# First expert started from the token blocks in SBUF, its weights loaded ahead of the routing, slot lists from two one-hot tables

## Chip, cores, metric

The kernel runs on one core of a Trainium2 chip. The metric is the device time of one execution in microseconds (us), the median of several runs.

## What is computed

Two transformer blocks on 512 tokens of width 1024, in float32. The part that the change touches is the mixture of experts of the first block: a router picks a group of four experts and two experts in it, and each token's result is the gated sum of the two.

```python
def hier_moe(h, w_rg, b_rg, w_re, b_re, w_gate, w_up, w_down):
    t = h.reshape(B * S, D)
    g_logits = (t @ w_rg) + b_rg
    g_idx = jnp.argmax(g_logits, axis=-1)
    e_sel = jnp.take_along_axis(e_logits, g_idx[:, None, None], axis=1)[:, 0]
    top_v, top_i = lax.top_k(e_sel, EXPERT_TOP_K)
    ...
    hid = jax.nn.silu(jnp.einsum('td,edf->tef', t, w_gate)) * jnp.einsum('td,edf->tef', t, w_up)
    hid = hid * gates.astype(hid.dtype)[:, :, None]
    y = jnp.einsum('tef,efd->td', hid, w_down)
```

There are 16 experts, each with 1024 x 512 gate and up weights and 512 x 1024 down weights.

## The kernel before

Products of weights are made from two parts of each operand, a rounded one (`hi`) and the rest (`lo`), in three matmuls of type float32r. ScalarE makes the `hi` part of a weight chunk (L160), VectorE the `lo` part (L164); plain float32 products and transposes occur in the routing. T = 512 tokens are NT = 4 blocks of P = 128; D = 1024 is KC = 8 chunks. Order is set by each engine's own instruction list and by semaphores that count.

**Routing.** When x is complete (L1885), TensorE turns the four token blocks to rows with products against the gain diagonals (`turn_scaled`, L1149), adds the shift (`add_shift`, L1234), and ScalarE evicts each block to `h_tok` (L710). SP stores each block to `h_dram` (L474). Meanwhile VectorE works out the two choices of each token in a chain of small linked steps (L1906 to L1941), TensorE counts for each expert how many tokens stand before a token (L1241, L1243), and VectorE makes from that `pos1`, the gates, and `tok_table` (six fields for each block and expert: token number, destination row, two gate parts and ones).

**Slots.** An expert takes up to 128 tokens in a round; the number of rounds is computed (`rounds`), and every engine reads it before its loop over rounds (`value_load`). This input needs one round. In it VectorE makes for each of the 16 experts a one-hot of positions (L2009), and TensorE multiplies it with the table (L1316, L1323) to get the list of tokens. `slot_numbers` (L2015 to L2025) turns the lists of experts 0 and 1, and later those of the rest, into row numbers. GpSimd gathers the rows of an expert from `h_dram` by an indirect DMA (L2406).

**Experts.** `turn_tokens` (L1257) transposes the gathered rows, ScalarE and VectorE split them into `e_hi` (L724) and `e_lo` (L1966). `expert_in` (L1267 to L1269) multiplies four weight chunks for the gate and four for the up half, `turn_hidden` (L1276) and `expert_down` (L1287 to L1289) follow one expert later. Results are evicted (L739) and scattered to `y_dram` by GpSimd (L2414). A ring of 12 buffers holds the weight chunks of 512 KB; SP loads them (L153) once a buffer's previous chunk is split, all inside its loop over rounds, behind the token stores. The ring lies over `h_hi`, `h_lo` and `raw`, which are free once x is complete. After the experts SP loads the rows of `y_dram`, VectorE adds the two choices (L2057) and TensorE turns them back (L1356).

## Time and profile before

| | us |
|---|---|
| median of 3 runs | 1859.93 |
| lowest and highest | 1853.70, 1861.27 |
| the profiled execution | 1857.48 |
| its span | 1855.7 |
| TensorE busy in the span | 1790.5 (96%) |
| VectorE, ScalarE, GpSimd busy | 1216.3, 913.3, 184.6 |

The profile is one execution. A window row gives each engine's busy time in a stretch, TensorE's granted clock as a share of full speed (1.00 is 2.4 GHz, 0.50 is 1.2 GHz) and what the DMA engines moved. PE is TensorE, DVE VectorE, ACT ScalarE, POOL GpSimd, SP SyncE. A matmul in float32 shows as two instructions.

### The profile page before, as it was taken

The numbers are of one execution on the slowest core, as the hardware profiler recorded it, in microseconds if no ns is written. First come the engines' busy times: TensorE is split into PE (matmuls) and PEld (weight loads), VectorE is DVE, ScalarE is ACT, GpSimd is POOL, SyncE is SP. The second block draws the span as 40 slices with busy tenths as digits, with TensorE's granted clock in tenths as the row PEclk, the third lists the DMA queues.
The fourth block names the chain that finished last, engine by engine and source line by source line (L and its number), as shares of the span: only waits on it lengthen the run. The fifth ranks groups of instructions, "written<-read, shape, count | busy, mean of one in ns | idle before, by whom it ended". The sixth has DMA issues, their size and how long they took to land.

```text
span 1855.7 us, 26079 instructions
## 1 busy us (share of the span) xinstructions
PE 1790.5 (96%) x8478; PEld 1393.8 (75%) x8478; DVE 1216.3 (66%) x1892; ACT 913.3 (49%) x1395; POOL 184.6 (10%) x219
## 2 busy tenths in 40 slices
PE   7999989899999879999999999999998999999999
PEld 5777667788888657776788888887774788888887
DVE  6777784798898672554577777224998567777422
ACT  3566752578788534564444444115665543444310
POOL 0000000222322100001000000000764000000000
PEclk9999999799999989999999999999999999999999
DMA  9533132999999452111233233331221223232321
GB/s 400 184 97 103 57 126 80 345 363 376 378 375 372 156 200 74 57 57 32 83 102 100 92 100 108 97 101 46 69 68 30 73 81 100 94 98 92 123 90 57
DMA packets 74099, 261.60 MB, mean 141 GB/s; under 512 B 10536, under 2 KB 10664, under 8 KB 72752
## 3 DMA queue, kind: packets, MB, share of 16 engines
q1 hardware_dynamic: 69424, 252.33, 38.8%
q0 software_dynamic: 4608, 8.40, 1.2%
q8 instruction: 40, 0.66, 0.1%
q14 instruction: 27, 0.22, 0.0%
HBM read 256.47 MB, written 12.60 MB: 145 GB/s over the span
## 4 chain that ended last, share of the span: by engine, by line
PE 86%; DVE 5%; DMA 3%; ACT 3%; issue 2%; SPq 0%; POOL 0%; DVEq 0%; POOLq 0%; ACTq 0%
PE ps L1027 19%; PE ps L1029 19%; PE ps L1028 19%; PE ps L1267 3%; PE ps L1269 3%; PE ps L1268 3%; PE ps L1660 2%; PE ps L1089 2%; PE ps L1287 2%; PE ps L1289 2%; PE ps L1288 2%; PE ps L1110 1%; DMA raw<-in_w_a 1%; PE ps L991 1%; PE ps L1480 1%
## 5 line engine op out<-in xcount | busy, mean ns | idle before, releaser
L1027 PE MATMUL ps<-h_hi,w_hi 128*128 128x512 f32 x1120 | 447.7, 400 | 1.3 <-DVEq L2273 1.3
L1029 PE MATMUL ps<-h_hi,w_lo 128*128 128x512 f32 x1120 | 436.8, 390 | 0.0
L1028 PE MATMUL ps<-h_lo,w_hi 128*128 128x512 f32 x1120 | 436.3, 390 | 0.0
L125 DVE TENSOR_TENSOR w_lo<-raw,w_hi 128x1024 fp32r<-128x1024 f32 x212 | 265.9, 1258 | 186.0 <-ACT w_hi L120 185.7
L120 ACT ACTIVATE w_hi<-raw 128x1024 fp32r<-128x1024 f32 x212 | 221.4, 1049 | 201.8 <-PE ps L1029 164.0
L1027 PEld LDWEIGHTS ps<-h_hi,w_hi 128*128 128x128 f32 x1120 | 210.4, 188 | 66.9 <-issue 24.3
L1029 PEld LDWEIGHTS ps<-h_hi,w_lo 128*128 128x128 f32 x1120 | 210.2, 188 | 44.5
L1028 PEld LDWEIGHTS ps<-h_lo,w_hi 128*128 128x128 f32 x1120 | 210.5, 188 | 43.7 <-issue 2.4
L164 DVE TENSOR_TENSOR w_lo<-ring,w_hi 128x1024 fp32r<-128x1024 f32 x128 | 149.5, 1218 | 28.0 <-ACT w_hi L160 28.0
L911 ACT ACTIVATE tmp<-ps,param 128x512 f32<-128x512 f32 x88 | 68.6, 780 | 185.6 <-DVE ps L2239 185.6
L2247 DVE SCALAR_TENSOR_TENSOR tmp<-ps,param,tmp 128x511 f32<-128x511 f32 (+1 forms) x176 | 131.8, 749 | 18.9 <-DVE tmp L2247 3.0
L1027 PE MATMUL ps<-gv_hi,w_hi 128*128 (+1 forms) x352 | 139.1, 395 | 0.0
L1029 PE MATMUL ps<-gv_hi,w_lo 128*128 (+1 forms) x352 | 139.0, 395 | 0.0
L1028 PE MATMUL ps<-gv_lo,w_hi 128*128 (+1 forms) x352 | 139.0, 395 | 0.0
L160 ACT ACTIVATE w_hi<-ring 128x1024 fp32r<-128x1024 f32 x128 | 128.6, 1055 | 11.8 <-PE ps L1269 11.8
L2383 POOL TENSOR_TENSOR pool_carrier<-const 128x1 f32<-128x1 f32 x74 | 35.3, 477 | 701.7 <-DVE x L2271 427.0
L2239 DVE TENSOR_TENSOR ps<-ps,const 128x512 f32<-128x512 f32 x88 | 61.2, 696 | 63.5 <-PE ps L1029 63.4
L2474 POOL TENSOR_TENSOR part<-prod,part 128x512 f32<-128x512 f32 x64 | 84.9, 1327 | 55.4 <-ACT prod L959 51.0
L1267 PE MATMUL ps<-w_hi,e_hi 128*128 128x512 f32 x192 | 78.4, 409 | 2.7 <-DVE e_lo L1966 2.7
L1029 PEld LDWEIGHTS ps<-gv_hi,w_lo 128*128 128x128 f32 x352 | 66.0, 187 | 16.2
L1027 PEld LDWEIGHTS ps<-gv_hi,w_hi 128*128 128x128 f32 x352 | 66.0, 187 | 16.1
L1028 PEld LDWEIGHTS ps<-gv_lo,w_hi 128*128 128x128 f32 x352 | 66.0, 187 | 16.1
(345 smaller groups left out, 2916.8 us busy)
## 6 DMA issues: line engine op xcount, KB each, us to landing
ring<-in_w_m SPq DMA_DIRECT2D x192, 512.0 KB, 5.6
raw<-in_w_b SPq DMA_DIRECT2D x180, 512.0 KB, 3.5
raw<-in_w_a SPq DMA_DIRECT2D x32, 512.0 KB, 3.8
ada_late<-in_ada_b SPq DMA_DIRECT2D x32, 512.0 KB, 4.6
ada<-in_ada_a SPq DMA_DIRECT2D x8, 1024.0 KB, 17.1
y_tok<-y_dram SPq DMA_DIRECT2D x8, 512.0 KB, 8.0
x<-in_x SPq DMA_DIRECT2D x2, 1024.0 KB
h_dram<-h_tok SPq DMA_DIRECT2D x4, 512.0 KB, 2.6
```

What stands on the lines that cost most here:

```text
L120: act.activation(self.hi[:, s, :], self.raw[:, s, :], ACT.Copy).then_inc(self.hi_done, 1)
L125: dve.tensor_tensor(self.lo[:, s, :], self.raw[:, s, :], self.hi[:, s, :].bitcast(F32), ALU.subtract).then_inc(self.lo_done, 1)
L160: act.activation(self.hi[c % PARTS_M], self.ring[:, c % RING], ACT.Copy).then_inc(self.hi_done, 1)
L164: dve.tensor_tensor(self.lo[c % PARTS_M], self.ring[:, c % RING], self.hi[c % PARTS_M].bitcast(F32), ALU.subtract).then_inc(self.lo_done, 1)
L911: act.activation(tmp[:, c], ps[:, c], ACT.Identity, scale=PR_at("ffn_w", it, 6, 3 * p + (f * 2 + val) * 3 * FC + 2), bias=PR_at("ffn_b", i ...
L1027: pe.matmul(dst, hi, a_hi, start=first, stop=False, skip_group_check=True)
L1028: pe.matmul(dst, hi, a_lo, start=False, stop=False, skip_group_check=True)
L1029: return pe.matmul(dst, lo, a_hi, start=False, stop=last, skip_group_check=True)
L1267: pe.matmul(ps[:, bank], e_hi[:, k], hi, start=(k == 0), stop=False, skip_group_check=True)
L2239: dve.tensor_tensor(ps[:, c], ps[:, c], r_kept, ALU.mult).then_inc(z_done, 1)
L2247: dve.scalar_tensor_tensor(out=tmp[:, c, back:], in0=ps[:, c, 0:T - back], scalar=PR_at("ffn_w", it, 6, 3 * p + (f * 2 + val) * 3 * FC + tap),
L2474: pool.tensor_tensor(part[:, p], prod[:, n % 4], part[:, p], ALU.add).then_inc(part_step, 1)
```

## The change

The table gets five fields for each of the two choices, block and expert: the token number, the destination row, a one, and two gate parts, each times the choice's expert one-hot. One one-hot for each choice (position of a token in its expert, whichever that is) times this table gives the lists of all 16 experts in 8 products with 80 columns. The first expert's tokens aren't gathered by a DMA: a third one-hot, `first_of`, is multiplied with `h_tok`, which gives them already turned, in two halves that are split one by one. SP issues the first expert's 12 weight loads ahead of the round count, with the four token stores among them, and waits for one more list at the end; GpSimd gathers from expert 1 on. Part of the last token block's products and ScalarE's exponentials stand earlier. The lists and one-hots of a next round are made at the end of the loop. `first_turned`, `first_hi` and `first_lo` are existing semaphores under new names; in SBUF the table and one-hots take room of `h_tok_at`, which lay unused. Cut to what the prediction speaks of:

```diff
--- before.py
+++ after.py
@@ -150,7 +151,8 @@
     def load(self, sp, base, i, c):
 
         sp.wait_ge(self.lo_done, base + (c + 1))
-        sp.dma_start(self.ring[:, c], self.src[bass.ds(i, 1), c]).then_inc(self.loaded[c][0], 16)
+        src = self.src[i:i + 1, c] if isinstance(i, int) else self.src[bass.ds(i, 1), c]
+        sp.dma_start(self.ring[:, c], src).then_inc(self.loaded[c][0], 16)
 
     def split_hi(self, act, base, lap, c):
 
...
@@ -469,18 +478,33 @@
             sp.dma_start(s_dram.rearrange("o (p k) -> p (o k)", k=KC), mod[:, 3 * KC:4 * KC]).then_inc(shift_in, 16)
             sp.wait_ge(shift_in, 16)
             sp.dma_start(shift_read[:], s_dram.broadcast_to([P, D])).then_inc(shift_in, 16)
-            for t in range(NT):
+
+            def store_tokens(t):
                 sp.wait_ge(h_tok_done, t + 1)
                 sp.dma_start(h_dram[t * P:(t + 1) * P], h_tok[:, t]).then_inc(h_stored, 16)
 
+            for c in range(8):
+                sm.load(sp, 0, 0, c)
+            store_tokens(0)
+            store_tokens(1)
+            for c in (8, 9):
+                sm.load(sp, 0, 0, c)
+            store_tokens(2)
+            store_tokens(3)
+            for c in (10, 11):
+                sm.load(sp, 0, 0, c)
             sp.wait_ge(rounds_done, 1)
             n_rounds = sp.value_load(rounds[0:1, 0:1], min_val=1, max_val=NT)
-            with sp.Fori(0, n_rounds) as r:
-                with sp.Fori(0, NE) as i:
-                    for c in range(RING):
-                        sm.load(sp, r * (12 * NE) + i * 12, i, c)
-
+            with sp.Fori(1, n_rounds * NE) as n:
+                e = n & (NE - 1)
+                sp.lower_val(e)
+                for c in range(RING):
+                    sm.load(sp, n * 12, e, c)
+
+            slots_end = n_rounds + 1
+            sp.lower_val(slots_end)
             sp.wait_ge(y_free, n_rounds * NE + 2)
+            sp.wait_ge(slots_done, slots_end)
             for t in range(NT):
                 for choice in range(2):
                     row = choice * T + t * P
@@ -709,9 +733,9 @@
                 act.wait_ge(h_turned, t + 1)
                 act.activation(h_tok[:, t].rearrange("p (b c) -> p b c", b=2), ps[:, turned_at(t):turned_at(t) + 2], ACT.Copy,
                                scale=r_tok[:, t:t + 1]).then_inc(h_tok_done, 1)
-                if t in (1, 2):
-                    act.wait_ge(route_sel, t)
-                    act.activation((r44[:, 1], r4[:, 9])[t - 1], (r44[:, 0], r4[:, 8])[t - 1], ACT.Exp).then_inc(route_exp, 1)
+                if t < 2:
+                    act.wait_ge(route_sel, t + 1)
+                    act.activation((r44[:, 1], r4[:, 9])[t], (r44[:, 0], r4[:, 8])[t], ACT.Exp).then_inc(route_exp, 1)
...
@@ -758,7 +782,11 @@
                 base, lap = r * (12 * NE), r * NE
                 for c in range(AHEAD_M):
                     sm.split_hi(act, base, lap, c)
-                expert_tokens_hi(r * NE)
+                    if c == 1:
+                        act.wait_ge(first_turned, r + 2)
+                        act.activation(e_hi[:, 0:KC // 2].rearrange("p k c -> p (k c)"), ps[:, 0], ACT.Copy).then_inc(first_hi, 1)
+                act.wait_ge(e_turned, r * NE + 3)
+                act.activation(e_hi[:, KC // 2:].rearrange("p k c -> p (k c)"), ps[:, 1], ACT.Copy).then_inc(e_hi_done, 1)
                 for c in range(8):
                     sm.split_hi(act, base, lap, c + AHEAD_M)
...
@@ -1237,6 +1265,9 @@
 
             add_shift(0)
             add_shift(1)
+            pe.wait_ge(h_tok_done, 1)
+            for k in range(KC // 2):
+                turn_scaled(k, 3)
             pe.wait_ge(route_sel, 3)
             pe.matmul(ps[:, RB, 0:NT * NE], C("before"), r16[:, 0], start=True, stop=False, skip_group_check=True)
             for d in range(1, NT + 1):
@@ -1244,10 +1275,19 @@
                                  stop=(d == NT), skip_group_check=True)
             last.then_inc(router_mm, 1)
             add_shift(2)
-            pe.wait_ge(h_tok_done, 1)
-            for k in range(KC):
+            for k in range(KC // 2, KC):
                 turn_scaled(k, 3)
             add_shift(3)
+
+            def slots_of(made):
+                pe.wait_ge(onehot_done, made)
+                for b in range(2 * NT):
+                    last = pe.matmul(ps[:, SSQ, 0:NE * FIELDS], onehot[:, b // NT, b % NT],
+                                     tok_table[:, b].rearrange("p e f -> p (e f)"), start=(b == 0), stop=(b == 2 * NT - 1),
+                                     skip_group_check=True)
+                last.then_inc(slots_done, 1)
+
+            slots_of(2)
 
             def turn_tokens(pair, n, s):
 
@@ -1257,9 +1297,25 @@
                     last = pe.transpose(ps[:, k // 4, k % 4 * P:(k % 4 + 1) * P], e_x[s][:, k * P:(k + 1) * P], C("ident"))
                 last.then_inc(e_turned, 1)
 
-            def expert_in(base, c0, bank):
+            def gather_first(r):
+
+                n = r * NE
+                pe.wait_ge(h_tok_done, NT)
+                pe.wait_ge(onehot_done, r * 3 + 3)
+                pe.wait_ge(e_lo_done, n + 1)
+                for b in range(2):
+                    for t in range(NT):
+                        for j in range(KC // 2):
+                            k = b * (KC // 2) + j
+                            last = pe.matmul(ps[:, b, j * P:(j + 1) * P], h_tok[:, t, k * P:(k + 1) * P], first_of[:, t].bitcast(F32),
+                                             start=(t == 0 and j == 0), stop=(t == NT - 1), skip_group_check=True)
+                    last.then_inc(e_turned if b else first_turned, 1)
+
+            def expert_in(base, c0, bank, second_half=None):
 
                 for b in range(4):
+                    if b == 2 and second_half is not None:
+                        pe.wait_ge(e_lo_done, second_half)
                     sm.ready(pe, base, c0 + b)
                     for j in range(2):
                         hi, lo = sm.parts(c0 + b, j, FE)
...
 
-                pe.wait_ge(y_evicted, r * NE + 1)
...
                 n = r * NE
-                turn_tokens(r * (NE // 2), n, 0)
-                with pe.Fori(6, NE // 2) as m:
-                    slots_of(m)
-                pe.wait_ge(e_lo_done, n + 2)
+                gather_first(r)
+                pe.wait_ge(first_lo, r + 5)
                 pe.wait_ge(silu_done, n + 1)
-                expert_in(r * (12 * NE), 0, 2)
+                expert_in(r * (12 * NE), 0, 2, n + 2)
                 pe.wait_ge(hid_done, n + 1)
                 expert_in(r * (12 * NE), 4, 3)
                 turn_tokens(r * (NE // 2), n + 1, 1)
                 with pe.Fori(0, NE // 2 - 1) as m:
                     pe.wait_ge(e_lo_done, r * NE + m * 2 + 3)
-                    expert_pe(r, m * 2 + 1, r * (NE // 2) + m + 1, 1)
+                    expert_pe(r, m * 2 + 1, r * (NE // 2 - 1) + m, 1)
                     pe.wait_ge(e_lo_done, r * NE + m * 2 + 4)
                     expert_pe(r, m * 2 + 2, r * (NE // 2) + m + 1, 0)
                 pe.wait_ge(e_lo_done, r * NE + (NE + 1))
                 expert_pe(r, NE - 1, 0, 1)
                 turn_hidden(r * NE + (NE - 1))
                 expert_down(r * (12 * NE), 12 * NE - 4, r * NE + (NE - 1))
+                slots_of(r * 3 + 6)
 
             pe.wait_ge(sm.used, n_rounds * (12 * NE) + PARTS_M)
...
@@ -1910,9 +1946,20 @@
                 link(dve.tensor_tensor(onehot_out, key, over(key_max, 2, T4), ALU.is_equal))
 
             TN, TE = [P, NT, NG + NE], [P, NT, NE]
-            tok = over(C("tok"), 2, TE)
-            link(dve.tensor_copy(tok_table[:].rearrange("p t e f -> p (t e f)"), ones[:, 0:1].broadcast_to([P, NT * NE * 6])))
...
 
-            link(dve.scalar_tensor_tensor(out=tok_table[:, :, :, 1], in0=r16[:, 2], scalar=float(T), in1=tok, op0=ALU.mult,
-                                          op1=ALU.add))
+            link(dve.tensor_tensor(fields(0), chosen_twice, for_both(numbers[:].rearrange("p f n t -> p f (n t)")), ALU.mult))
+            link(dve.tensor_copy(tok_table[:, :, :, 2], chosen))
+            dve.wait_ge(route_exp, 2)
+            link(dve.tensor_reduce(out=r4[:, 2], in_=r44[:, 1], axis=AX.X, op=ALU.add))
+            link(dve.scalar_tensor_tensor(out=r4[:, 10], in0=r4[:, 9], scalar=1.0, in1=r4[:, 2], op0=ALU.add, op1=ALU.mult))
+            link(dve.reciprocal(gates[:, 0], r4[:, 10]))
+            link(dve.tensor_tensor(gates[:, 1], gates[:, 0], r4[:, 9], ALU.mult))
+            gate = gates[:].rearrange("p n t -> p (n t)")
+            link(dve.tensor_copy(gate_parts[:, 0], gate))
+            link(dve.tensor_tensor(gate_parts[:, 1], gate, gate_parts[:, 0].bitcast(F32), ALU.subtract))
+            link(dve.tensor_tensor(fields(3), chosen_twice, for_both(gate_parts[:].bitcast(F32)), ALU.mult))
 
             dve.wait_ge(router_mm, 2)
+            link(dve.scalar_tensor_tensor(out=pos_of[:].rearrange("p n t e -> p n (t e)"),
+                                          in0=ps[:, RB, 0:NT * NE].unsqueeze(1).broadcast_to([P, 2, NT * NE]), scalar=1.0,
+                                          in1=r16[:, 1:3].rearrange("p n t e -> p n (t e)"), op0=ALU.add, op1=ALU.mult))
+            link(dve.tensor_reduce(out=pos[:].rearrange("p n t -> p (n t)"), in_=pos_of[:].rearrange("p n t e -> p (n t) e"),
+                                   axis=AX.X, op=ALU.add))
+
+            link(dve.tensor_tensor(pos_first, pos_of[:, 0, :, 0], pos_of[:, 1, :, 0], ALU.add))
+
+            def slots_wanted():
+                for n in range(2):
+                    dve.tensor_tensor(onehot[:, n], over(pos[:, n], 2, [P, NT, P]), over(iota_r[:], 1, [P, NT, P]),
+                                      ALU.is_equal).then_inc(onehot_done, 1)
+
+            def first_wanted():
+                dve.tensor_tensor(first_of[:], over(pos_first, 2, [P, NT, P]), over(iota_r[:], 1, [P, NT, P]),
+                                  ALU.is_equal).then_inc(onehot_done, 1)
+
+            dve.wait_ge(iota_done, 1)
+            slots_wanted()
             link(dve.tensor_reduce(out=rounds_f[:, 0:1], in_=ps[:, RB, NT * NE:(NT + 1) * NE], axis=AX.X, op=ALU.max))
             link(dve.tensor_scalar(rounds_f[:, 1:2], rounds_f[:, 0:1], float(P), 1.0, ALU.is_gt, ALU.add))
             for n in (2, 3):
                 link(dve.scalar_tensor_tensor(out=rounds_f[:, n:n + 1], in0=rounds_f[:, 0:1], scalar=float(n * P),
                                               in1=rounds_f[:, n - 1:n], op0=ALU.is_gt, op1=ALU.add))
             dve.tensor_copy(rounds[:], rounds_f[:, 3:4]).then_inc(rounds_done, 1)
-            dve.wait_ge(route_exp, 2)
-            link(dve.tensor_reduce(out=r4[:, 2], in_=r44[:, 1], axis=AX.X, op=ALU.add))
-            link(dve.scalar_tensor_tensor(out=r4[:, 10], in0=r4[:, 9], scalar=1.0, in1=r4[:, 2], op0=ALU.add, op1=ALU.mult))
-            link(dve.reciprocal(r4[:, 11], r4[:, 10]))
-            link(dve.tensor_tensor(r4[:, 3], r4[:, 11], r4[:, 9], ALU.mult))
-            link(dve.tensor_tensor(pos1[:], r16[:, 1], over(r4[:, 11], 2, TE), ALU.mult))
-            link(dve.tensor_tensor(r16[:, 1], r16[:, 2], over(r4[:, 3], 2, TE), ALU.mult))
-            link(dve.tensor_tensor(r16[:, 2], pos1[:], r16[:, 1], ALU.add))
-            link(dve.tensor_copy(tok_table[:, :, :, 2], r16[:, 2]))
-            link(dve.tensor_tensor(tok_table[:, :, :, 4], r16[:, 2], tok_table[:, :, :, 2].bitcast(F32), ALU.subtract))
-            link(dve.scalar_tensor_tensor(out=pos1[:], in0=ps[:, RB, 0:NT * NE].rearrange("p (t e) -> p t e", t=NT),
-                                          scalar=1.0, in1=r16[:, 0], op0=ALU.add, op1=ALU.mult))
+            first_wanted()
 
             def expert_tokens_lo(n):
...
                 base = r * (12 * NE)
-                with dve.Fori(2, 6) as m:
-                    slots_of(m)
-                slots_of(6)
+                dve.wait_ge(slots_done, r + 1)
+                dve.wait_ge(idx_ready, r * (2 * NE - 1) + 1)
+                dve.tensor_copy(slot_table[:].rearrange("p e f -> p (e f)"), ps[:, SSQ, 0:NE * FIELDS]).then_inc(slot_idx, 1)
+                dve.wait_ge(slot_idx, r * 3 + 1)
+                dve.scalar_tensor_tensor(out=slot_rows_f[:], in0=over(slot_table[:, :, 2], 1, [P, 2, NE]), scalar=-4096.0,
+                                         in1=slot_table[:, :, 0:2].rearrange("p e f -> p f e"), op0=ALU.mult, op1=ALU.add)\
+                   .then_inc(slot_idx, 1)
+                dve.wait_ge(slot_idx, r * 3 + 2)
+                dve.tensor_scalar(slot_rows[:], slot_rows_f[:], 4096.0, None, ALU.add).then_inc(slot_idx, 1)
+                dve.tensor_tensor(slot_gate[:], slot_table[:, :, 3], slot_table[:, :, 4], ALU.add)
                 sm.split_lo(dve, base, 0)
-                slots_of(7)
-                expert_tokens_lo(r * NE)
-                for c in range(1, 4):
-                    sm.split_lo(dve, base, c)
-                dve.wait_ge(slots_done, r * NE + (NE + 2))
-                slot_numbers(SSQ, 2, NE, 3)
-                dve.tensor_scalar(iota_r[:], iota_r[:], float(P), None, ALU.add).then_inc(iota_done, 1)
-                dve.wait_ge(iota_done, r + 2)
+                sm.split_lo(dve, base, 1)
+                dve.wait_ge(first_hi, r + 2)
+                dve.tensor_tensor(e_lo[:, 0:KC // 2].rearrange("p k c -> p (k c)"), ps[:, 0],
+                                  e_hi[:, 0:KC // 2].bitcast(F32).rearrange("p k c -> p (k c)"), ALU.subtract).then_inc(first_lo, 1)
+                sm.split_lo(dve, base, 2)
+                dve.wait_ge(e_hi_done, r * NE + 1)
+                dve.tensor_tensor(e_lo[:, KC // 2:].rearrange("p k c -> p (k c)"), ps[:, 1],
+                                  e_hi[:, KC // 2:].bitcast(F32).rearrange("p k c -> p (k c)"), ALU.subtract).then_inc(e_lo_done, 1)
+                sm.split_lo(dve, base, 3)
                 for c in range(4, 8 + AHEAD_M):
                     sm.split_lo(dve, base, c)
                 hidden(base, 7, r * NE, 0)
@@ -2049,6 +2094,10 @@
                     expert_dve(r, e)
                 expert_dve(r, NE - 1)
                 hidden_lo(r * NE + (NE - 1))
+                dve.tensor_scalar(iota_r[:], iota_r[:], float(P), None, ALU.add).then_inc(iota_done, 1)
+                dve.wait_ge(iota_done, r + 2)
+                first_wanted()
+                slots_wanted()
 
...
@@ -2392,7 +2441,6 @@
             pool.wait_ge(rounds_done, 1)
             n_rounds = pool.value_load(rounds[0:1, 0:1], min_val=1, max_val=NT)
             pool.wait_ge(zeroed, 2)
-            pool.wait_ge(h_stored, 16 * NT)
 
             def column(ap, e):
...
@@ -2403,6 +2451,8 @@
                 pool.tensor_copy(src_e[:, s:s + 1], column(slot_src, e)).then_inc(idx_ready, 1)
                 pool.wait_ge(idx_ready, copied)
                 settle(1)
+                if isinstance(e, int) and e == 1:
+                    pool.wait_ge(h_stored, 16 * NT)
                 pool.indirect_dma_start(e_x[s][:], None, h_dram, bass.IndirectOffsetOnAxis(ap=src_e[:, s:s + 1], axis=0),
                                         bounds_check=T - 1, oob_is_err=False).then_inc(fetched[s], 16)
```

## Rows read from the trace of the kernel before

**Rows 1.** Stage windows: from:to, length, each engine's busy us (instructions), granted clock, DMA share, GB/s.
```profile
324.00:326.50 2.50, 0.07 (x1) 0.00 (x0) 0.93 (x3) 1.11 (x1) 0.00 (x0) 1.00 0.19 77
326.50:350.50 24.00, 21.60 (x84) 20.07 (x85) 18.28 (x30) 9.16 (x9) 5.87 (x11) 0.50 0.91 355
...
360.00:362.60 2.60, 0.00 (x0) 0.00 (x0) 2.06 (x3) 2.60 (x3) 1.54 (x4) 1.00 1.03 411
400.00:600.00 200.00, 200.00 (x930) 162.94 (x929) 178.01 (x165) 161.69 (x178) 53.54 (x85) 1.00 0.99 376
...
637.50:640.50 3.00, 3.00 (x8) 2.32 (x8) 0.00 (x0) 0.00 (x0) 0.31 (x2) 0.50 0.14 56
```

**Rows 2.** Chain of waits, two experts: start, us, what.
```profile
603.74 0.44 PE ps L1276 x4
...
621.84 0.44 PE ps L1276 x4
```

**Rows 3.** Chain of waits, from the routing's end to the first expert matmul.
```profile
324.00 0.23 DVE pos L1961
...
325.80 0.70 DVE onehot L2009
...
331.68 8.09 DMA e_x<-h_dram,src_e
...
339.81 1.97 PE ps L1257 x8
...
345.28 0.79 PE ps L1267
```

**Rows 4.** Timeline of TensorE, experts 0 and 1: start, us, instruction [idle before, releaser].
```profile
350.55 0.39 PE L1267 MATMUL ps<-w_hi,e_hi 128*128 128x512 f32 x1
...
358.92 1.04 PE L1257 MATMUL ps<-const,e_x 128*128 128x128 f32 x8
362.62 0.50 PE L1267 MATMUL ps<-w_hi,e_hi 128*128 128x512 f32 x1 [2.66 <-DVE e_lo L1966]
```

**Rows 5.** Timeline of the token blocks on TensorE and ScalarE.
```profile
315.66 0.59 PE L1234 MATMUL ps<-e_y,tmp 128*128 128x512 f32 x1
...
317.46 0.43 PE L1241 MATMUL ps<-r,const 128*128 128x64 f32 x2 [1.21 <-DVE r L1939]
...
320.40 1.05 PE L1149 MATMUL ps<-e_silu,x 128*128 128x128 f32 x8
...
321.29 1.06 PE L1149 MATMUL ps<-e_hid,x 128*128 128x128 f32 x8
...
324.10 1.11 ACT L710 ACTIVATE h_tok<-ps,e_y 128x1024 f32<-128x1024 f32 x1 [2.30 <-PE ps L1234]
```

**Rows 6.** Timeline of VectorE: a step of 64 and one of 512 elements.
```profile
317.18 0.23 DVE L1939 TENSOR_TENSOR r<-r 128x64 f32<-128x64 f32 x1
...
327.66 0.69 DVE L2009 TENSOR_TENSOR onehot<-pos,iota_r 128x512 fp32r<-128x512 f32 x1 [0.57 <-PE ps L1316]
```

**Rows 7.** Instructions on the ring (ns min/median/max, first and last start), and ScalarE's table load.
```profile
L160 ACT ACTIVATE w_hi<-ring x128: 1040/1054/1064, 332.0 to 627.9; 128x1024 fp32r<-128x1024 f32 x128
L164 DVE TENSOR_TENSOR w_lo<-ring,w_hi x128: 1212/1218/1237, 339.7 to 629.8; 128x1024 fp32r<-128x1024 f32 x128
...
330.73 1.28 ACT L160 ACT_TABLE_LOAD   x1 [5.51 <-DMA ring<-in_w_m]
```

**Rows 8.** When x is ready (timeline), the weight loads' landing, and the stores' (DMA issues).
```profile
307.94 0.75 DVE L1885 SCALAR_TENSOR_TENSOR x<-ps,mod,x 128x512 f32<-128x512 f32 x1 [6.62 <-PE ps L1029]
...
DMA to landing us min/median/max: 3.7/5.6/13.6
...
h_dram<-h_tok SPq DMA_DIRECT2D x4, 512.0 KB, 2.6
```

**Rows 9.** The gathers' time to landing.
```profile
DMA to landing us min/median/max: 3.6/6.1/8.4
```

**Rows 10.** Waits between 634 and 656 us: engine, line, awaited, us, times, longest.
```profile
PE ps L1356 <- DVE y_tok L2057: 11.6, 1, 11.6
```

92 lines of the change are left out of this document (33 added, 59 removed).

## Prediction

> **What bounds the kernel now.** I read the stage windows first: they show where TensorE is full and where not. Over 400 to 600 us TensorE is busy for 200.00 of 200 us at full clock [rows 1]. The experts there repeat every 621.84 - 603.74 = 18.10 us [rows 2], which is 72 matmuls of 0.233 us plus transposes, so the expert loop is bound by TensorE. Nothing ahead of it changes its rate; what comes ahead only moves its start. The part that isn't bound by work is 324 to 362.6 us, the way into the experts. The chain of waits over it [rows 3] is a relay of small steps: the loop's entry on VectorE, a one-hot, its products, the slot numbers, GpSimd's preparations, an 8.09 us gather, the transposes, and only then the first expert matmul at 345.28. TensorE's granted clock is 0.50 (the 1.2 GHz level) for the 24 us from 326.5 to 350.5, after 2.5 us with almost no work, and comes back at 350.5, after 12 of the expert matmuls ran at it [rows 1, 3, 4]. The last wait of the stage is at 358.9 to 362.6, while the tokens of expert 1 are turned and split [rows 4]. From 362.62 on TensorE has no gap until the last expert's tail near 634. So the change is worth the distance by which that 362.62 moves, as long as no later expert meets a new wait.
>
> **The change, part by part.** I follow TensorE and take each other engine as cover.
>
> (a) The last token block. The products of tokens 384 to 511 (L1149, 8 products in 16 instructions) stand behind the counts and after the third shift; they start at 320.40 and 321.29, so 8 instructions take 0.89 us, 0.111 each [rows 5]. Half of them, 0.89 us, go ahead of the counts. TensorE is through with the second block at 315.66 + 0.59 = 316.25 and waits until 317.46 for the chosen experts, so they fit into 1.21 us and cost nothing; without that cover they would delay the counts by 0.89 us. The last block's eviction then starts at 323.2 instead of 324.10 and, with its 1.11 us, is done at 324.3.
>
> (b) VectorE's new tables. They must be done when TensorE wants them. Prices: 64 elements 0.23 us, 512 elements 0.69 us [rows 6]; by the line through them 128 take 0.30 and 256 take 0.43, and a linked step adds about 0.04. From 317.3, behind the sum of the chosen experts [rows 6]: two field products of 256 (0.47 each), a copy of 128 (0.33), four gate steps and two splits of tiny size (0.2 each, 1.2), the positions and their sum (0.33 each), the first expert's positions (0.2). That is 3.3 us, 320.7. Two one-hots of 512 (1.3) end at 322.0, the five tiny steps of the round count (0.9) at 322.9, the first expert's one-hot at 323.6. The exponentials stand one block earlier on ScalarE, the second behind the second block's eviction (316.3 + 1.11 [rows 5]) and not behind the third's, so it is there before 318 and VectorE does not wait for it. TensorE wants the first two one-hots at 323.2 and the third at 324.3 or later: 1.2 and 0.7 us of cover. If the five-word stride made the 256-element steps cost 0.69 each, 0.5 us would be gone and still nothing late.
>
> (c) Slot lists. Sixteen one-hots and 64 products, in the old loop until 345.28, become 8 products with 80 columns. No row shows 80 columns in this type. L1149's instructions have 128 columns and are nearest: 8 x 0.111 = 0.9 us; as pairs they would be 1.8. I take 1.0 (bounds 0.9 and 1.8): 324.2.
>
> (d) Loop entry. VectorE needs 1.57 us from the end of its last operation (324.23) to the first of the loop (325.80), most of it loading the round count [rows 3]. ScalarE and TensorE do the same. For TensorE the trace doesn't show it alone: bounds are 0 (its sequencer does it while the queued products run) and 1.5 us. Rounds are known at 322.9, before its queue is empty, so I take the middle, 0.7 us behind 324.3: the gather starts at 325.0.
>
> (e) Gather by products. 2 banks x 4 token blocks x 4 chunks = 32 float32 products. Each such product is two instructions in the trace (the 8 of L1149 are 16), so 64, with L1149's shape: 64 x 0.111 = 7.1 us and 0.2 for the first one's way in, 7.3, ending at 332.3 [rows 5]. It replaces the DMA gather (8.09) and the transposes (1.97 at half clock) [rows 3]. Bounds: 7.1, and 8.4 if each takes the 0.131 that the busy 1.05 us of 8 give; at half clock, 14.6.
>
> (f) First expert's input products. ScalarE enters at 324.3 + 1.5, table load 1.28, then splits of 1.05 and subtractions of 1.22 on VectorE [rows 7]. By that order the first token half is split at about 331.4, behind two weight chunks and ahead of 332.3, and the second at about 333.7, when TensorE wants it at 335.1; the later chunks are ready 1.6 us or more before their use. So 48 matmuls (8 chunks x 6) run without a gap: 48 x 0.233 = 11.2 us, to 343.5. Before they took 358.92 - 345.28 = 13.6: the first 12 took 350.55 - 345.28 = 5.3, 0.44 each, the other 36 took 8.4, 0.233 each [rows 3, 4].
>
> (g) Expert 1. Turn, ScalarE's copy, VectorE's subtraction: the same 362.62 - 358.92 = 3.7 us as before [rows 4], to 347.2. VectorE's other splits up to chunk 11 end at about 344.3 and its hidden product at 345.0, before that subtraction wants to start at 345.5; 0.5 us to spare.
>
> Sum: 362.62 - 347.2 = 15.4 us earlier, carried through the expert loop to the end.
>
> (h) SP. It now issues 12 loads of 512 KB once x is ready, at 307.94 + 0.75 = 308.7, and not behind the round count [rows 8]; the four token stores stand among them, with 8 loads ahead of the first. Before, a store landed in 2.6 us [rows 8]. 14 transfers of 0.524 MB up to the last store at 355 GB/s (326.5 to 350.5 us, loaded [rows 1]) are 1.48 us each: 20.7 us, plus the 2.6 of a store, 332.0. GpSimd holds only the gather of expert 1 for it; issue 0.6 later, landing 8.4 at most [rows 9]: 341.0, wanted at 343.5. Cover is 2.5 us. Chunks 0 to 9 land before ScalarE wants them; expert 1's loads are issued from 329 on, one as each chunk is split, 12 ahead of use as before. The Trainium skill, "DMA: Bandwidth & Descriptors", section on queues, rings and completion order, says that each DMA engine takes one ring's descriptors in ring order. By that rule the stores can't pass the weights, and this would give the late gather among the rivals; the rows of before hold no store behind loads that could confirm it.
>
> (i) Loop end. Three one-hots (2.0 us) on VectorE behind the last hidden split and 8 products behind TensorE's last expert matmul. TensorE has no work for 11.6 us there, since it waits for VectorE's sum of the loaded rows [rows 10]; SP's added wait is met within 1 us of the last expert matmul, before the last result is even scattered. Cost nothing; without that cover, 3 us.
>
> Total: 1857.48 - 15.4 = 1842.1. That profiled execution lies 2.4 us below the median of the three runs, inside their 1853.7 to 1861.3.
>
> **Rivals.**
> 1. The clock falls. For: 2.5 us without work preceded the fall at 326.5, and a short gap near 634 preceded the 3 us at 0.50 from 637.5 [rows 1]. Against: in the new order TensorE is without work for at most about 1.5 us there, and the 2.6 us at 360 were followed by no fall. If it falls ahead of the gather and comes back after 12 of the 48 matmuls, as before: +7.3 and 12 x 0.2 = +2.4, 1851.8.
> 2. Slower than before: the same fall, but the clock stays down for 24 us as it did at 326.5. Then the gather takes +7.3 and the 48 matmuls run at 0.44 (+9.9), 17.2 in all, expert 1 starts at 364.4 and the time is 1859.3. It is slower than before once more than 15.4 us are lost, that is when at least 40 of the 48 matmuls run at half clock.
> 3. The gather of expert 1 comes late. With a landing of 13.6 us, the longest of the weights [rows 8], it is there at 346.2: +2.7, 1844.8.
> 4. The change hides what is hidden anyway: if ScalarE's entry or VectorE's tables end last, TensorE stalls ahead of the products. Entries a further 2 us late would give 1844.
> 5. The gap of 2 us at 634 falls on another moment of the clock: the 3 us at half clock there cost 1.6. 8 matmuls at 0.44 and not 0.233. It may be spared (1840.5), or the 2.6 us gap ahead of expert 1 may bring a fall (+2.4, 1844.5).
>
> **How the numbers follow.** Forecast, with the small variants 4 and 5 around it: 0.80. Rival 1: 0.08. Rival 2: 0.03. Rival 3: 0.09. Low end: TensorE's entry free (0.7), the end gap spared (1.6), and 3.8 for the scatter of runs (the lowest lies 3.8 below the profiled one): 1836. High end: entry of 1.5 (+0.8), products at 0.131 (+1.1), rival 3 or a fall ahead of expert 1 (+2.5), slower slot lists (+0.8), the highest run's 3.8 above: 1851.1; rounded up into rival 1, 1852. A measurement here tells 0.5%, 9.3 us, from no change. Faster by over 0.5%: the forecast and rival 3 but for what the scatter takes, 0.83. Within: rivals 1 and 2 and that scatter, 0.14. Slower: 0.03, a form of rival 2 that costs 24 us, for which no row speaks.
>
> **What would show it.** Right: in the profile after, the 64 gather instructions start at 324.2 to 325.7 and take 7 to 8.4 us; the first expert matmul is at about 332.3; granted clock 1.00 from 312 to 350; weight loads begin at about 309; expert 1's first matmul is at about 347.2; the period of an expert stays 18.1. Wrong: a granted clock of 0.50 between 325 and 345; TensorE waiting on the expert 1 gather or on a weight chunk; an onehot wait ahead of 324; any gap in 350 to 600; a longer distance from the last expert matmul to the first transposes of the sum.

## The result, and the profile of the changed kernel

| | before | changed | predicted |
|---|---|---|---|
| median, us | 1859.78 | 1839.14 | 1842.1 |
| lowest to highest | 1853.7 to 1861.3 | 1838.6 to 1841.4 | 1836 to 1852 |
| ratio to before | 1 | 0.9901 (0.9882 to 0.9919) | 0.992 |
| profiled execution | 1857.48 | 1838.63 | |
| its span | 1855.7 | 1836.8 | |

The medians differ by 20.6 us and the profiled executions by 18.9, where the sum gave 15.4. The forecast's time, 1842.1, counts from the profiled execution of before, which lies 2.3 us below before's median here; so the measured time is 3.0 us below the forecast, while the gain of the medians is 5.2 us above it. The table follows both profiles along the same instructions of TensorE.

| TensorE, us | before | changed | gained so far |
|---|---|---|---|
| first router product (L1137, now L1165) | 308.74 | 308.26 | 0.5 |
| expert 1's first matmul | 362.62 | 346.75 | 15.9 |
| first matmul after the last expert's last wait | 635.95 | 620.50 | 15.5 |
| first transpose of the summed rows | 654.96 | 638.01 | 17.0 |
| first product of the next stage | 677.50 | 659.35 | 18.2 |
| end of the span | 1855.7 | 1836.8 | 18.9 |

From the router product to expert 1 it is 53.88 us before and 38.49 after, 15.39 less: the forecast's 15.4. What lies over it came elsewhere, and the rest of this section and the runs say how much of that is the change's.

The chain of waits of the changed kernel over the routing and the first expert (start, us, what):

```profile
322.72 1.12 ACT h_tok L734
323.84 0.80 issue
324.64 7.41 PE ps L1310 x64
332.05 0.24 PE ps L1323
...
343.21 0.89 PE ps L1297 x8
344.12 1.03 ACT e_hi L748
345.18 1.24 DVE e_lo L2030
...
346.75 0.71 PE ps L1323
```

The relay of [rows 3] is gone. Between the last token block and the first expert matmul stand an entry of 0.80 us and the 64 gather instructions, and from 332.05 to 343.21 the 48 matmuls follow without a gap. The stage windows, with the columns of [rows 1]:

```profile
324.00:325.50 1.50, 0.86 (x7) 0.86 (x8) 0.52 (x3) 0.75 (x1) 0.00 (x0) 1.00 1.04 426
325.50:334.00 8.50, 8.50 (x69) 8.09 (x68) 5.67 (x8) 6.94 (x9) 2.39 (x8) 1.00 1.00 391
334.00:345.00 11.00, 10.08 (x48) 8.07 (x46) 10.37 (x10) 9.14 (x10) 1.96 (x4) 1.00 0.91 323
346.80:350.40 3.60, 3.60 (x9) 2.83 (x10) 1.87 (x2) 1.00 (x2) 0.00 (x0) 0.53 1.04 380
400.00:600.00 200.00, 200.00 (x934) 163.67 (x933) 179.41 (x168) 161.78 (x178) 52.51 (x82) 1.00 0.99 376
```

Where [rows 1] had 24 us at a granted clock of 0.50, it is 1.00 from 308 to 346.8. In this profile the clock falls behind the wait ahead of expert 1 (0.53 in 346.8 to 350.4), which it did not do in before's; e5 and e10 take that up. The experts fill TensorE as before, with 934 instructions in 200 us where there were 930.

Timeline of VectorE and TensorE: a step of the new table, the one-hots, the lists:

```profile
316.83 0.62 DVE L1988 TENSOR_TENSOR tok_table<-r,numbers 128x256 fp32r<-128x256 f32 x1
...
320.52 1.29 DVE L2011 TENSOR_TENSOR onehot<-pos,iota_r 128x512 fp32r<-128x512 f32 x2
...
322.12 1.38 PE L1285 MATMUL ps<-tok_table,onehot 128*128 128x80 f32 x8
...
322.58 0.68 DVE L2015 TENSOR_TENSOR first_of<-pos_first,iota_r 128x512 fp32r<-128x512 f32 x1
```

GpSimd's timeline at the gather of expert 1, and the DMA issues between 305 and 350 us:

```profile
331.47 1.23 POOL L2456 DMA_INDIRECT e_x<-h_dram,src_e  x1 [5.00 <-DMA h_dram<-h_tok]
```

```profile
ring<-in_w_m SPq DMA_DIRECT2D x26, 512.0 KB, 7.1
h_dram<-h_tok SPq DMA_DIRECT2D x4, 512.0 KB, 7.0
```

GpSimd waits 5.00 us for the last token store. A store takes 7.0 us among the weight loads, where it took 2.6 before [rows 8]; the gather of expert 1 is nevertheless issued at 331.47, 11.7 us ahead of the transposes that read it, and the gathers of this stretch land in 7.3.

### The profile page after: what moved, and what is told of

Same layout as the page of the kernel before. It is cut to its first block, busy times and chain, and to the rows that moved or that the text cites. A ratio compares the mean times of both kernels' runs of the same rounds, so it can differ in the third digit from the quotient of the medians.

```text
span 1836.8 us, 25944 instructions
## 1 busy us (share of the span) xinstructions
PE 1779.8 (97%) x8486; PEld 1385.9 (75%) x8486; DVE 1209.8 (66%) x1882; ACT 913.2 (50%) x1396; POOL 183.0 (10%) x215
## 4 chain that ended last, share of the span: by engine, by line
PE 85%; DVE 6%; issue 4%; ACT 3%; DMA 2%; DVEq 0%; SPq 0%; POOL 0%; POOLq 0%; ACTq 0%
PE ps L1055 19%; PE ps L1057 18%; PE ps L1056 18%; PE ps L1323 3%; PE ps L1324 3%; PE ps L1325 3%; PE ps L1117 2%; PE ps L1345 2%; PE ps L1343 2%; PE ps L1344 2%; PE ps L1696 1%; PE ps L1138 1%; DMA raw<-in_w_a 1%; PE ps L1019 1%; DVE w_lo L126 1%
## 5 line engine op out<-in xcount | busy, mean ns | idle before, releaser
L2296 DVE SCALAR_TENSOR_TENSOR tmp<-ps,param,tmp 128x511 f32<-128x511 f32 (+1 forms) x176 | 131.8, 749 | 17.5 <-DVE tmp L2296 3.1
```

The costliest lines, as they stand in the source:

```text
L2296: dve.scalar_tensor_tensor(out=tmp[:, c, back:], in0=ps[:, c, 0:T - back], scalar=PR_at("ffn_w", it, 6, 3 * p + (f * 2 + val) * 3 * FC + tap),
```

## The experiments

Each run is read at two places: the median against before on the same chip, and the distance D from the first router product to expert 1's first matmul, which leaves out what executions scatter elsewhere. D is 53.88 us before and 38.49 in the changed kernel. "Per expert" is the distance between the hidden transposes of two experts, as in [rows 2].

| | median, us | ratio (95%) | D, us | per expert, us |
|---|---|---|---|---|
| e1 loads late | 1846.15 | 0.9941 (0.9924 to 0.9958) | 43.24 | 18.02 |
| e2 DMA gather | 1850.38 | 0.9957 (0.9940 to 0.9973) | 47.47 | 18.02 |
| e3 lists only | 1848.41 | 0.9951 (0.9934 to 0.9967) | 47.42 | 18.02 |
| e4 before, loads early | 1855.49 | 0.9988 (0.9976 to 1.0000) | 51.85 | 18.09 |
| e5 changed again | 1839.61 | 0.9907 (0.9892 to 0.9922) | 38.57 | 18.02 |
| e6 gather twice | 1847.73 | 0.9951 (0.9936 to 0.9966) | 45.75 | 18.02 |
| e7 tiles moved | 1843.06 | 0.9922 (0.9908 to 0.9935) | 38.55 | 18.10 |
| e8 clock kept | 1841.18 | 0.9915 (0.9901 to 0.9928) | 38.71 | 18.02 |
| e9 clock kept again | 1839.84 | 0.9909 (0.9895 to 0.9922) | 38.67 | 18.02 |
| e10 changed a third time | 1842.12 | 0.9916 (0.9902 to 0.9930) | 38.58 | 18.02 |

Before has 1857.81 on the chip of e1 to e4, 1857.61 on that of e5 to e8 and 1857.0 on that of e9 and e10.

The theory: the gain is the way into the experts, and its largest part is the product gather in place of the store, gather, transposes and half clock. The first rival: the fresh slot lists alone bring most of it. The second: the early loads are mere cover, or on the contrary carry a share.

### Loads back behind the round count (e1)

```diff
-            for c in range(8):
-                sm.load(sp, 0, 0, c)
-            store_tokens(0)
...
+            for t in range(NT):
+                store_tokens(t)
             sp.wait_ge(rounds_done, 1)
             n_rounds = sp.value_load(rounds[0:1, 0:1], min_val=1, max_val=NT)
+            for c in range(RING):
+                sm.load(sp, 0, 0, c)
```

> The changed kernel, but the first expert's 12 weight loads are issued behind the round count (about 324.2 us) and the four token stores ahead of them. Theory (the gain is the relay that is gone; the early loads only make room for it): weight chunk 1 then lands at about 329.5, the first token half is split at 332.3 in place of 330.1, and TensorE's first expert matmul moves from 331.8 to about 332.3; later chunks stay just ahead of TensorE. 0.5 to 1.5 us slower than the changed kernel, about 1840. Rival (the early loads carry the gain, since they start 16.7 us earlier): 10 us or more slower, 1849 or above.

Measured: D is 43.24, 4.75 us more than in the changed kernel. That is a miss. TensorE's timeline of this run, and behind it the chain of waits:

```profile
336.05 0.49 PE L1317 MATMUL ps<-w_hi,e_hi 128*128 128x512 f32 x1 [3.03 <-DVE e_lo L2076]
...
348.88 1.04 PE L1291 MATMUL ps<-const,e_x 128*128 128x128 f32 x8
```

```profile
324.26 1.12 ACT h_tok L728
...
331.20 13.28 DMA ring<-in_w_m
...
348.57 1.07 ACT m_hi L162
...
351.47 1.22 DVE e_lo L2024
...
353.03 0.49 PE ps L1317
```

The router product is at 309.79 here and at 308.26 in the changed kernel, so times are taken from it. TensorE is late by itself: the first expert matmul stands at 26.26 us and not at 23.54 (2.72 more), since the split of the first token half waits behind two weight chunks; behind that wait of 3.03 us the clock falls (0.54 in 337.5 to 341.2), and from the first matmul to the turn it is 12.83 and not 11.25 (1.58 more). From the turn to expert 1 it is 4.15 and not 3.70 (0.45 more).

The chain says what ended last. The tenth of the 12 loads, issued one behind another on SP, lands at 344.5. In the list of VectorE's work the splits of the first expert's chunks stand ahead of the subtraction `e_lo` for expert 1, so that subtraction begins 41.68 us behind the router product and not 36.92. No matmul stands on the chain from that landing to expert 1, so a TensorE in time would by this chain not have started expert 1 sooner; no run tries it. The early loads are worth 4.75 us once the gather is fast. The expectation priced the first matmul's delay at 0.5 us, and neither the fall nor the place of expert 1's subtraction behind the splits.

### First expert gathered by DMA, loads early or late (e2, e3)

```diff
-                gather_first(r)
+                pe.wait_ge(h_tok_done, NT)
+                pe.wait_ge(fetched[0], r * (NE // 2) * 16 + 16)
+                pe.wait_ge(e_lo_done, n + 1)
+                for k in range(KC):
+                    last = pe.transpose(ps[:, k // 4, k % 4 * P:(k % 4 + 1) * P], e_x[0][:, k * P:(k + 1) * P], C("ident"))
...
-                for e in range(1, 4):
+                for e in range(4):
                     gather(r, e, e % 2, done + (e + 1))
```

e3 has the edit of e1 as well, so that of the change the lists are left, with the earlier products and exponentials and the tokens' split in two halves.

> The changed kernel, but expert 0's tokens come by an indirect DMA and transposes as before; early loads and slot lists stay. Theory: the token stores stand behind eight weight loads and land at about 331.4, so the gather starts at 331.5 and lands 6 to 8 us later; the first expert matmul is at about 341.8 in place of 331.8, and the granted clock falls meanwhile (2.4 us more): 10 to 12.5 us slower than the changed kernel, 1849 to 1852. Rival (the DMA gather hides, since the slot rows are there 4 us earlier): at most 4 us slower, 1843.

> Only the slot lists of the change: two one-hots and the table over experts, with expert 0 gathered by DMA and its loads behind the round count. Theory: stores land at 326.5, gather from 326.9 with 12 loads in the queues beside it, 8 us, to 335; first expert matmul about 338.8 (before: 345.3), clock fallen as before: 6 to 7 us faster than the kernel before, about 1848 to 1851, and faster than the kernel with early loads and DMA gather, since there the stores wait. Rival (all lies in the clock or in the loads): within 2 us of the kernel before.

The chain of waits of e2, and behind it that of e3:

```profile
324.85 1.12 ACT h_tok L734
325.99 6.60 DMA h_dram<-h_tok
...
333.48 4.51 DMA e_x<-h_dram,src_e
...
340.71 0.79 PE ps L1323
341.50 0.43 PE ps L1324
```

```profile
322.55 1.12 ACT h_tok L728
323.69 2.58 DMA h_dram<-h_tok
...
327.16 8.05 DMA e_x<-h_dram,src_e
...
337.94 0.79 PE ps L1317
338.72 0.43 PE ps L1318
```

In both D is 47.4, 9.0 us more than with products and 6.4 less than before. The store and the gather take 11.1 us in one and 10.6 in the other: with early loads the last store is slow (6.60) and the gather quick (4.51), with late loads it is the other way round (2.58 and 8.05). TensorE has no work for 12.48 and 12.00 us ahead of the transposes, and behind that both run their first eleven to thirteen matmuls at 0.43 us, half clock. That D agrees within 0.05 us is partly luck: e3's first expert matmul is 0.47 us earlier, measured from the router product, and its 48 matmuls take 0.42 longer. The expectation that e3 is the faster one, since the stores don't wait, is a miss by D; its median is 2.0 us lower, within what medians of one kernel scatter. The Trainium skill, "DMA: Bandwidth & Descriptors", section on queues, rings and completion order, says that an engine works through one ring's descriptors in ring order; a last store of 6.60 us behind loads against 2.58 with none ahead fits it, though these runs don't tell that order from busy engines that are merely shared.

### The early loads added to the kernel before (e4)

```diff
+            for c in range(8):
+                sm.load(sp, 0, 0, c)
+            store_tokens(0)
...
             sp.wait_ge(rounds_done, 1)
             n_rounds = sp.value_load(rounds[0:1, 0:1], min_val=1, max_val=NT)
-            with sp.Fori(0, n_rounds) as r:
```

> The kernel before with the early loads alone (the stores among them as in the changed kernel). Theory: nothing on the relay waits for weights; the stores land about when the first gather is issued (331.7), and that gather has fewer loads beside it (6 in place of 8.1 us): 0 to 2 us faster than before, 1857 to 1859. Rival (the early loads carry the gain): 8 us or more faster, 1851 or below.

Measured: D falls by 2.03 us, the median by 2.3; the interval ends at 1.0. That is the upper edge of what was expected. The chain goes through the old relay still:

```profile
331.23 0.70 DVE onehot L2022
...
343.85 1.88 PE ps L1336 x8
...
346.49 0.43 PE ps L1281
```

The gather is no longer on it. In before TensorE made slot products while it waited and stood idle for the gather only at the very end:

```profile
339.81 1.97 PE L1257 MATMUL ps<-const,e_x 128*128 128x128 f32 x8 [0.73 <-DMA e_x<-h_dram,src_e]
```

So a gather that lands sooner (4.7 us here, 8.09 before) can give little more than 0.73 us before the products and their one-hots end last. The first expert matmul comes 1.13 us earlier, measured from the router product (35.41 against 36.54), and the 48 matmuls take 12.74 and not 13.64.

By D the change comes apart so: the lists with the earlier token block alone 6.46 us; the product gather without early loads another 4.18; the early loads then 4.75; together 15.39. Of the 6.46 some 0.9 are probably the token block, since e3's chain goes through its store and its eviction ends 15.59 us behind the router product where before had 16.48; no run separates the two, nor what the split in halves gives. In another order the parts have other prices: the early loads first 2.03, then the lists 4.38, then the product gather 8.98. So the theory's "largest part" holds for the gather only where the loads are early, and neither rival holds alone. The early loads are worth nothing with a DMA gather (e2 against e3, 0.05) and 4.75 with the product gather: the two parts need each other.

### The gather made twice (e6), the changed kernel beside it (e5)

```diff
-                for b in range(2):
+                for b, again in ((0, 0), (0, 1), (1, 0), (1, 1)):
...
-                    last.then_inc(e_turned if b else first_turned, 1)
+                    if again:
+                        last.then_inc(e_turned if b else first_turned, 1)
```

> The changed kernel itself, as the base for the three that follow. In its profile the first expert-1 matmul comes 38.5 us after the first router product behind the complete x (308.26 to 346.75 in the first profile), the last expert's wait 273.75 us later (or 272.2 if the clock doesn't fall at the start of expert 1). About 1839.

> The changed kernel with the 64 gather instructions issued twice (the second pass gives the same sums). Theory (the gather's products are on the path, ScalarE and VectorE wait for them): the first expert matmul moves by the 7.2 us that 64 instructions took, 1846. Rival (weight splits on ScalarE and VectorE set the start, the products run beside them): less than 4 us, 1843 or below.

```profile
325.39 0.88 issue
326.27 14.55 PE ps L1310 x128
```

128 instructions take 14.55 us where 64 took 7.41, 0.114 each. D grows by 7.2 us and the median by 8.1. So the products stand on the path with their whole length, and the rival of weight splits that set the start falls. A longer gather can't show how little the rest lies behind it. For that there is e1, and in the changed kernel VectorE was free only 0.51 us before it could begin the subtraction for expert 1, near the 0.5 of the prediction.

### The shorter period of an expert (e7)

The changed kernel needs 18.02 us for an expert and before 18.09, though its loop is the same. TensorE's timeline of before, then of the changed kernel, first and last of the 12 gate and up matmuls that read `m_hi` or `m_lo`:

```profile
582.70 0.39 PE L1267 MATMUL ps<-m_hi,e_hi 128*128 128x512 f32 x1
...
585.26 0.39 PE L1269 MATMUL ps<-m_lo,e_hi 128*128 128x512 f32 x1
```

```profile
585.46 0.39 PE L1323 MATMUL ps<-m_hi,e_hi 128*128 128x512 f32 x1
...
587.97 0.40 PE L1325 MATMUL ps<-m_lo,e_hi 128*128 128x512 f32 x1
```

Eleven steps take 2.56 us in one and 2.51 in the other, 0.233 and 0.228 each. The matmuls that read `w_hi` and `w_lo` take 0.233 in both. By the tiles that the change makes smaller, `m_hi` and `m_lo` lie 416 words (1664 bytes of each partition) lower. e7 puts them back with a tile that nobody reads:

```diff
+            sb("m_at", [P, 416], stack=st)
             m_hi = sb("m_hi", [P, PARTS_M - SLOTS, 1024], F32R, stack=st)
```

> The changed kernel with 416 unused words ahead of m_hi, so that m_hi and m_lo lie where they lay before the change. Theory (where these two lie sets the pitch of the matmuls that read them, 0.229 us in the changed kernel and 0.233 before): an expert takes 18.09 us and not 18.02, the stretch of the experts 273.3 us where no clock fall is in it and not 272.2; 1.1 us slower, 1840. Rival (the shorter period comes from the other order of transfers): period stays 18.02 and the time 1839.

The chain of waits of e7, then of the changed kernel, at the hidden transposes:

```profile
573.27 0.44 PE ps L1333 x4
...
591.37 0.44 PE ps L1333 x4
```

```profile
570.36 0.44 PE ps L1332 x4
...
588.37 0.44 PE ps L1332 x4
```

The period goes back to 18.10. Fifteen experts times 0.07 are 1.1 us of the gain which come from where tiles lie. The stretch from expert 1 to the last expert's wait agrees: 273.33 us before and 272.22 in e5, both without a fall of the clock; 274.64 in e7 and 273.75 in the changed kernel, both with one. The median of e7 is 3.4 us above e5's and its 1843.06 a miss against the expected 1840; the excess lies within what the changed kernel's own medians scatter (e10). The unread tile moves `e_x1` and `e_y1` too, which lie behind `m_lo`; that `m_hi` and `m_lo` matter is read from the matmuls, of which only those that read them change their step. Why the address matters isn't settled by these runs.

### The clock kept up (e8, e9) and the changed kernel a third time (e10)

The fall behind expert 1's wait is in the changed kernel's first profile and in e10, and not in e5, which is the same kernel. The windows of e5 and e10:

```profile
346.80:350.40 3.60, 3.02 (x13) 2.48 (x14) 2.72 (x4) 1.93 (x2) 0.13 (x1) 1.00 1.04 379
```

```profile
346.80:350.40 3.60, 3.04 (x7) 2.46 (x8) 2.48 (x3) 0.93 (x2) 0.11 (x1) 0.57 1.02 390
```

With the fall the stretch from expert 1 to the last expert's wait took 273.72 to 273.75 us (changed, e2, e10), without it 272.21 to 272.22 (e1, e3, e5, e6): 1.5 us. The length of the wait doesn't decide it: in e1 it is 3.12 us and no fall follows, in e5 2.67 and none, in e10 2.67 and one. e8 gives TensorE products that nobody reads in four of its waits (`unread(n)` issues n of them):

```diff
                 turn_tokens(r * (NE // 2), n + 1, 1)
+                pe.wait_ge(silu_done, n + 2)
+                unread(2)
...
                 turn_hidden(r * NE + (NE - 1))
+                unread(2)
...
             pe.wait_ge(y_evicted, n_rounds * NE + 1)
+            unread(11)
...
+                if t:
+                    for _ in range(4):
+                        pe.matmul(ps[:, 2, (NT - 1) * P:], C("ident"), const[:, 0:P], start=True, stop=True,
+                                  skip_group_check=True)
```

> The changed kernel with matmuls whose results nobody reads in the waits of TensorE: two 512-column float32 products ahead of expert 1 and two ahead of the last down products, eleven ahead of the sum's transposes and four of 128 columns between its token blocks. Theory (the half clock after these waits costs 1.5 us behind the first, 1.5 behind the second where it falls, and about 2 us in the transposes and norm sums after the experts): granted clock 1.00 throughout 340 to 655 us, 2 to 4 us faster than the changed kernel, 1835 to 1837. Rival (the half-clock work stands beside transfers and VectorE, so nothing is won, and the extra products delay the real ones): within 1 us of the changed kernel or slower.

> The kernel of the clock-kept run once more, in more rounds, beside the changed kernel on the same chip. If the 2.1 to 2.4 us that its profile gained between the first router product and the next block's first product are lasting, and the loss ahead of the router belonged to that one execution, its median is 2 to 2.5 us below the changed kernel's. If the chip gives elsewhere what it takes here (a fall ahead of the router in its place), the two medians agree within 1 us, and the profile has a granted clock of 0.80 to 0.85 in 220 to 242 us again.

> The changed kernel itself, as the other side of the run before. Its median is 1838.5 to 1840.5. Its profile has a granted clock of 1.00 in 220 to 242 us if the fall there is a matter of the kernel, and either if it is a matter of the execution; expert 1's first matmul comes 38.4 to 38.6 us behind the first router product.

The window 620 to 680 us of e9, then of e10:

```profile
620.00:680.00 60.00, 54.62 (x354) 37.05 (x353) 36.75 (x54) 20.16 (x29) 1.96 (x7) 1.00 0.49 172
```

```profile
620.00:680.00 60.00, 44.53 (x302) 32.45 (x303) 38.39 (x56) 19.32 (x29) 3.05 (x9) 0.86 0.48 172
```

The clock stays at 1.00 where it was 0.86 around the sum of the rows. From the first router product to the first product of the next stage e8 takes 348.65 us and e9 349.59, the changed kernel 351.09, 350.75 and 350.72: 1.1 to 2.4 us less. The medians don't show it reliably: 1.6 us above the changed kernel beside e5, 2.3 below it beside e10. So the local gain is real in the profiles and as a time it is not told from zero; the expected 2 us and more in the time were missed in e8 and met in e9 (2.3). e10's median, 1842.12, is itself above the 1838.5 to 1840.5 expected of it. The window 220 to 242 us, ahead of everything that differs, of e8, then of e9:

```profile
220.00:242.00 22.00, 15.80 (x76) 10.05 (x72) 15.39 (x45) 11.81 (x31) 0.00 (x0) 0.84 0.14 47
```

```profile
220.00:242.00 22.00, 15.75 (x95) 10.72 (x92) 17.00 (x50) 14.10 (x37) 0.00 (x0) 1.00 0.15 48
```

e8 and e9 are one kernel, and only one of them has the fall; it starts the router at 310.41 and 308.22. The other profiles bear it out: where this window has 1.00 (before, changed, e3, e5, e9, e10) the router starts at 308.08 to 308.81, where it has 0.92 (e1, e2, e4, e6, e7) at 309.79 to 310.39. A fall there is a matter of the execution, and not what the filling gives back.

## Why the prediction came out as it did

**What held, step by step.** (a) The last block's eviction ends 15.58 us behind the first router product (323.84 - 308.26) and was expected at 15.56 (324.3 - 308.74). (b) VectorE's tables are in time: two one-hots done at 321.81, the first expert's at 323.26. The 256-element steps cost 0.62 us and not 0.43, near the text's own fallback of 0.69, and the cover that was named took it. (c) The lists start at 322.12 and their group covers 1.38 us; with the eviction ending at 323.84 they are not on the path, so their price didn't matter. (d) The entry is 0.80 us (0.80 to 0.98 in all profiles with early loads and the product gather, 0.24 in e1 with late ones, for which no run shows the reason) where 0.7 was taken out of 0 to 1.5. (e) The gather is 7.41 against 7.3, and e6 shows that its length is on the path. (f) The 48 matmuls take 11.16 (343.21 - 332.05) against 11.2. (g) From the turn to expert 1 it is 3.54 (346.75 - 343.21) against 3.7. The errors of (d) to (g), +0.1, +0.1, 0.0 and -0.2, cancel. The last is in part one of reading: by the timeline, from which the 3.7 was taken, the turn begins at 343.05 and the way is 3.70, as before.

(h) The stores came later, as worked out: GpSimd was free to gather for expert 1 at 331.5 where the text had 332.6, the ring order holding. Where the step was too short is the value of the early loads. It treated them as cover for the chunks; e1 shows that they carry 4.75 of the 15.39 us, by the first token half's split, a fall of the clock and, last of all, VectorE's list. The number for the whole was right since the sum was made with the loads early; read as prices of parts, it would have been wrong.

(i) The 8 products at the loop's end run at 626.20 for 0.98 us, ahead of this wait, and cost nothing:

```profile
626.20 0.98 PE L1285 MATMUL ps<-tok_table,onehot 128*128 128x80 f32 x8
638.01 1.94 PE L1392 MATMUL ps<-const,y_tok 128*128 128x128 f32 x8 [10.83 <-DVE y_tok L2106]
```

**Where it was off.** The sentence that failed is that the distance is carried unchanged through the expert loop to the end, together with the forecast that the period of an expert stays. Beyond the 15.4 the profiled pair gained 3.5 us:
- 1.1 us from the shorter period, shown by e7; no row of before could tell it, but that tiles move in SBUF stood in the diff and had no bound in the range.
- minus 1.5 us for the fall behind expert 1's wait, the second half of rival 5, priced there at 2.4. It comes in some executions only: in the changed kernel's first profile and e10, in e2, e4 and e7, and not in before, e1, e3, e5 and e6. Whether the change makes it more frequent, one profile of before can't tell.
- 1.5 us between the last expert and the sum, where the clock fell in before's profile and not in this one: the first half of rival 5. e2, e5 and e7 have the 19.0 us of before there, e1, e3, e4, e6 and e10 the 17.5 of the changed kernel, so it is not the change's.
- 1.2 us between the sum and the next stage (22.5 before, 21.3 after). e4 has before's loops and 21.1, so this isn't the change's either.
- 0.5 us ahead of the router and 0.7 behind it all, in code that is the same.

What the change owns is 15.4 + 1.1 = 16.5 us by the profiles. The medians gave 20.6, 18.0 and 14.9 in three comparisons, 17.8 on the mean: 16.5 and a scatter of some 3 us either way. The first result's 5.2 us over the forecast are thus 1.1 of mechanism and otherwise scatter, and e10's 1842.12 is the forecast by chance as much as by reckoning.

**The rivals.** 1 and 2 (a fall ahead of the gather) didn't occur in any profile of the product gather; the 1.14 us without work ahead of 324.64 were followed by no fall. e2 and e3 show what they would have looked like, matmuls at 0.43. 3 (late gather of expert 1) stayed away: issued at 331.47 and landing in some 7.3, the tokens were there about 4.4 us ahead of 343.21, where the text had 2.5 of cover by the longest landing. 4 did not occur. 5 occurred, in both halves, by execution: the end gap's cost was spared in this profile and paid in e5, and the fall ahead of expert 1 came in this profile and not in e5.

## What to carry to other kernels

When a chain of waits is replaced, price the parts in the combination in which they will run: a load moved ahead was worth 0.05 us with the slow gather, 2.03 in the old relay and 4.75 with the fast one. Look also at what stands behind the late work in an engine's list, here the next expert's subtraction behind the splits of the last chunks. An engine that waits for one thing while it has work of another kind, as TensorE did for the gather, gains little more than the idle rest (0.73 us) when that one thing comes sooner. A distance between two landmarks in the same profile is a sharper measure than the time: it held to 0.1 us (38.49, 38.57, 38.58) where medians of the same kernel spread over 3 us.

## What the runs showed of the hardware

- A float32r matmul of 128x512 started every 0.233 us or every 0.228 depending on where its moving operand lay, and moving two tiles by 1664 bytes changed it both ways (changed kernel, e7). Matmuls whose moving operand lay elsewhere kept 0.233.
- The same kernel met a fall of the clock in one execution and not in another, at three places: behind a wait of 2.67 us ahead of expert 1 (changed against e5), behind the last expert (e5 against changed), and in 220 to 242 us (e8 against e9). Each costs about 1.5 to 2.2 us (273.75 against 272.22, 19.05 against 17.51, 310.41 against 308.22). A wait of 3.12 us at the first place was followed by none (e1).
- A 512 KB store took 2.6 us with no loads ahead of it and 6.6 to 7.2 with loads ahead; the gather behind it took 8.05 us while the engines moved 407 GB/s (e3) and 4.51 while they moved 213 (e2), so the sum hardly changed.
